# Dealing out a depthwise convolution of 31 taps over GpSimd, VectorE and ScalarE, and moving weight loads to another queue

## The reference

```
u = rms_norm(h) * (1 + scale) + shift
p = u @ w_in                       # q, k, v, za, glu (a and g), zc
q, k = rope_2d(norm per head)      # 8 query heads, 2 key heads, 64 wide
attn = softmax over 2304 keys (256 context + 2048 own) * silu(za)
glu  = a * sigmoid(g)              # 512 channels
conv = depthwise conv of glu, width 31, padding 15, + bias
conv = silu(layer_norm(conv)) @ w_pw + b_pw, times silu(zc)
h = h + gate * ([attn, conv] @ w_out)
```

## Time and profile before

| | us |
|---|---|
| median of 3 runs | 3052.08 (3051.74 to 3052.36) |
| the profiled execution | 3046.05 |
| its span | 3044.2 |
| projections, first turn to last | 1209.3 to 1895.6 |
| attention, first score matmul of step 0 | 1967.7 |

### The profile page before, as it was taken

How to read it: one execution, slowest core, us unless ns; L and a number is a source line. 1 busy time by engine, 2 the same in 40 slices (tenths; PEclk the granted TensorE clock), 3 DMA queues, 4 the chain that set the end, 5 groups by cost and what they waited for, 6 DMA issues and landing times. The chain is left out here.

```text
span 3044.2 us, 35493 instructions
## 1 busy us (share of the span) xinstructions
PE 2615.0 (86%) x11647; PEld 1777.7 (58%) x11647; DVE 1814.0 (60%) x2830; ACT 1092.1 (36%) x1875; POOL 793.3 (26%) x365
## 2 busy tenths in 40 slices
PE   8599899999999962767989797299999999975998
PEld 1277677777777751645767675144454445433776
DVE  0106423533532524698898888677777777746564
ACT  0234433333332413241414132144454445433332
POOL 0033300000000101532111111166566656642000
PEclk9799999999999985888999999599999999987999
DMA  8275664454355341746555554411111111124334
GB/s 307 94 250 167 225 218 143 155 186 164 134 193 193 101 152 59 258 150 228 188 185 202 183 204 157 99 27 26 33 26 28 27 33 26 28 71 149 117 117 148
DMA packets 230581, 414.82 MB, mean 136 GB/s; under 512 B 19607, under 2 KB 112397, under 8 KB 230204
## 3 DMA queue, kind: packets, MB, share of 16 engines
q1 hardware_dynamic: 230096, 413.13, 40.9%
q10 hardware_dynamic: 364, 0.13, 0.0%
HBM read 306.87 MB, written 97.94 MB: 133 GB/s over the span
## 5 line engine op out<-in xcount | busy, mean ns | idle before, releaser
L1694 DVE TENSOR_REDUCE att_mx<-att_bank_m 128x1 f32<-128x512 f32 (+1 forms) x640 | 365.5, 630 | 111.6 <-PE att_bank_m L1558 107.6
L1662 ACT ACTIVATE att_p_f<-att_bank_s 128x512 f32<-128x512 f32 x576 | 317.7, 598 | 288.0 <-PE att_bank_s L1599 281.0
L412 PE MATMUL gla_bank_g<-gla_a_hi,gla_w_hi 128*128 128x512 f32 x1024 | 416.1, 406 | 4.1 <-POOL gla_w_lo L365 3.1
L412 PE MATMUL gla_bank_g<-gla_a_hi,gla_w_lo 128*128 128x512 f32 x1024 | 403.7, 394 | 0.0
L412 PE MATMUL gla_bank_g<-gla_a_lo,gla_w_hi 128*128 128x512 f32 x1024 | 403.7, 394 | 0.0
L1543 POOL TENSOR_TENSOR att_den<-att_den,att_p_f 128x1024 f32<-128x1024 f32 x160 | 379.4, 2371 | 34.1 <-ACT att_p_f L1662 22.0
L1333 DVE SCALAR_TENSOR_TENSOR proj_conv_acc<-proj_conv_in,proj_conv_w,proj_conv_acc 128x528 f32<-128x528 f32 x508 | 383.2, 825 | 0.3
L1196 PE MATMUL proj_bank_g<-proj_u_hi,proj_w_hi 128*128 128x512 f32 x704 | 302.8, 430 | 74.9 <-DMA proj_w_lo<-scratch_w_lo 37.8
L1196 PE MATMUL proj_bank_g<-proj_u_lo,proj_w_hi 128*128 128x512 f32 x704 | 283.5, 403 | 0.0
L1196 PE MATMUL proj_bank_g<-proj_u_hi,proj_w_lo 128*128 128x512 f32 x704 | 282.6, 401 | 0.0
L1573 PE MATMUL att_bank_o<-att_p_f,att_v 128*64 128x512 f32 x1152 | 268.4, 601 | 0.0
(11 more groups left out here) (322 smaller groups left out, 4195.4 us busy)
## 6 DMA issues: line engine op xcount, KB each, us to landing
gla_w_hi<-scratch_w_hi SPq DMA_DIRECT2D x96, 512.0 KB, 3.7
gla_w_lo<-scratch_w_lo SPq DMA_DIRECT2D x96, 512.0 KB, 4.7
proj_w_hi<-scratch_w_hi SPq DMA_DIRECT2D x66, 512.0 KB, 3.9
proj_w_lo<-scratch_w_lo SPq DMA_DIRECT2D x66, 512.0 KB, 5.3
scratch_w_hi<-gla_w_hi SPq DMA_DIRECT2D x32, 512.0 KB, 3.2
scratch_w_lo<-gla_w_lo SPq DMA_DIRECT2D x32, 512.0 KB, 4.2
mod_wslab<-in_ada_w SPq DMA_DIRECT2D x6, 2048.0 KB, 11.2
mod_wslab<-in_w_mod SPq DMA_DIRECT2D x6, 2048.0 KB, 8.1
```

Source lines behind the costliest of these rows:

```text
L412: last = pe.matmul(banks[s % 2][:], w[:, k, :], a[:, k, :], start=(k == 0 and n == 0), stop=(k == KT - 1 and n == 2))
L1662: act.activation(p_f[:, kt, :], S[kt % SBANKS][:], ACT.Exp, scale=float(HD) ** -0.5).then_inc(p_done, 1)
L1694: dve.reduce_max(mx[:, qt, n:n + 1], M[p % MBANKS][:, 0:min(TB, KEYS - TB * n)], AX_X).then_inc(mx_read, 1)
```

## The change

In `projections`:
- Chunk 0 of the convolution goes to GpSimd, 31 taps a block, each a tensor_scalar into `prod` and a tensor_tensor add (the first tap only the former), dealt by POOL_TAPS_OF_TURN. Chunks 1 and 2 stay on VectorE, 512 wide (528 in the last block), 62 a block, 11 of them carried to the next block's first two turns, none in block 0. Chunk 3 is only written to scratch as `conv_u`, with its weights.
- `u_hi` is rounded and biased on ScalarE (`round_u`) instead of VectorE; `scale_h` comes one turn earlier. The work for a block after the last is gone.
- The pairs are loaded from ScalarE's queue (`load_pair`), after ScalarE has waited for the turn that frees the tile, and the rings have four places.
- SP stores three parts of the convolution apart: GpSimd's at turn 21, VectorE's at turn 3, `conv_u` at turn 9.

In `attention`: chunk 3, one tap a step over all 2048 tokens in steps 0 to 30. ScalarE multiplies four parts of 512 at tiles 4, 6, 8 and 13; GpSimd adds once, 128x2048, behind its six denominator adds. The lists of ScalarE and GpSimd are written out, not loops. The result is stored at the end.

```diff
-    TAPS_OF_TURN = [10, 10, 8] + [0] * 2 + [8] * 5 + [2] * 6 + [8] * 4 + [6] * 2
-    CARRIED = sum(TAPS_OF_TURN[:4])
+    RING = 4
+    NTAP = 2 * TAPS
+    POOL_C, DVE_C, LATE_C = 0, 1, 3
+    TAPS_OF_TURN = [6, 5] + [0] * 4 + [7] * 3 + [5] * 2 + [0] * 5 + [2, 3, 3, 4, 5, 3]
+    CARRIED = sum(TAPS_OF_TURN[:6])
+    POOL_TAPS_OF_TURN = [0] * 2 + [2] * 2 + [1] * 4 + [3, 2, 3, 2, 3] + [1] * 6 + [2] * 2
...
                         if j == 20 and b + 2 < NB:
                             sp.wait_ge(u_done, UP + b * 8 + 16)
...
+                        if j == 21:
+                            sp.wait_ge(pool_taps, UP + (b + 1) * TAPS)
+                            sp.dma_start(conv_y[:, POOL_C, ds((b + 1) * TB, window(b))],
+                                         conv_acc[:, POOL_C, 0:window(b)]).then_inc(pool_conv_stored, 16)
+                        if j == 9:
+                            sp.wait_ge(glu, UP + b * 4 + 4)
+                            sp.dma_start(d["conv_u"][:, ds(b * TB, TB)], vraw).then_inc(late_stored, 16)
...
+                                if k == 0:
+                                    pool.tensor_scalar(acc, conv_src(b, POOL_C, k), conv_w[:, POOL_C, 0:1], None, ALU.mult).then_inc(pool_taps, 1)
+                                else:
+                                    pool.tensor_scalar(prod[:, 0:window(b)], conv_src(b, POOL_C, k), conv_w[:, POOL_C, k:k + 1], None,
+                                                       ALU.mult).then_inc(pool_prod, 1)
+                                    pool.wait_ge(pool_prod, UP + b * (TAPS - 1) + k)
+                                    pool.tensor_tensor(acc, acc, prod[:, 0:window(b)], ALU.add).then_inc(pool_taps, 1)
...
+                def load_pair(n):
+                    j = n % NW
+                    if n < NW + RING:
+                        act.wait_ge(w_kept[n % RING], UP + 32 * (n // RING))
+                    if n < 2 * NW:
+                        act.wait_ge(w_kept[j % RING], UP + 32 * (j // RING + 1))
+                    for part, tile in (("w2_hi", w_hi[n % RING]), ("w2_lo", w_lo[n % RING])):
+                        act.dma_start(tile[:].rearrange("p k n -> p (k n)").bitcast(F32), d[part][j]).then_inc(pair_landed[n % RING], 16)
...
+                def round_u(b, k):
+                    act.wait_ge(hm, UP + b * 8 + k + 1)
+                    act.activation(u_hi[b % 2][:, k, :], hbuf[:, k, :], ACT.Identity, bias=modv[:, 1, k:k + 1]).then_inc(u_done_hi, 1)
...
                         act.wait_ge(proj, UP + b * NW + j + 1)
+                        if NW <= b * NW + j + RING < NB * NW:
+                            load_pair(b * NW + j + RING)
...
+    MUL_AT = (4, 6, 8, 13)
...
+                def tap(k):
+                    pool.wait_ge(conv_mul, UP + NB * (k + 1))
+                    if k:
+                        pool.wait_ge(conv_taps, UP + k)
+                    former = conv_prod[:, 0, :, :] if k == 1 else conv_acc[:].rearrange("p (a b) -> p a b", a=NB)
+                    if k == 0:
+                        pool.sem_inc(conv_taps, 1)
+                    else:
+                        pool.tensor_tensor(conv_acc[:].rearrange("p (a b) -> p a b", a=NB), former, conv_prod[:, k % 2, :, :], ALU.add).then_inc(conv_taps, 1)
...
                         pool.tensor_tensor(den[s][:], pair(0) if j == 1 else den[s][:], pair(j), ALU.add).then_inc(den_pool, 1)
-                steps(pool, body)
+                    if i < TAPS:
+                        tap(i)
...
+                    if k > 1:
+                        act.wait_ge(conv_taps, UP + k - 1 + (k == 2))
+                    act.activation(conv_prod[:, k % 2, part, :], conv_in[:, k + TB * part:k + TB * (part + 1)], ACT.Copy,
+                                   scale=conv_w[:, k:k + 1]).then_inc(conv_mul, 1)
```

More of the change, by code:

```diff
@@ L1029, in projections @@
         w_landed = [sem(f"w_landed{s}") for s in range(2)]
[L1030 to L1031 removed]
+        pair_landed = [sem(f"pair_landed{s}") for s in range(RING)]
+        w_kept = [sem(f"w_kept{s}") for s in range(RING)]
         w_rounded, w_rest, proj, evac = sem("w_rounded"), sem("w_rest"), sem("proj"), sem("evac")
@@ L1650, in finish, with multiply @@
                     act.activation(o_hi[:], O[HD:P, :], ACT.Copy).then_inc(o_hi_done, 1)
-                def body(i, s, g, before, after):
+                def multiply(k, part):
+                    if k == 0 and part == 0:
+                        act.wait_ge(conv_landed, UP + 32)
+                        act.wait_ge(conv_cleared, UP + 2)
+                    if k > 1:
+                        act.wait_ge(conv_taps, UP + k - 1 + (k == 2))
+                    act.activation(conv_prod[:, k % 2, part, :], conv_in[:, k + TB * part:k + TB * (part + 1)], ACT.Copy,
+                                   scale=conv_w[:, k:k + 1]).then_inc(conv_mul, 1)
+                round_q(0, 0)
+                act.wait_ge(ones_landed, UP + 16)
+                for g in range(NKV):
+                    act.activation(k_b[g][HD:HD + 1, :], ones[HD:HD + 1, 0:1].broadcast_to([1, KEYS]), ACT.Copy).then_inc(ones_row, 1)
+                round_k(0)
+                round_q(1, 1)
+                for g in range(1, NKV):
+                    round_k(g)
+                read_row(0, 0)
+                for i in range(STEPS):
+                    s = i % 2
+                    before, after = i if i else None, i + 1 if i + 1 < STEPS else None
                     for kt in range(NKT):
@@ L1664, in body @@
                             finish(i - 1, 1 - s)
-                        if kt == 11 and not (isinstance(i, int) and i + 2 >= STEPS):
+                        if kt == 11 and i + 2 < STEPS:
                             round_q(i + 2, s)
@@ L1668, in body @@
                             read_row(i + 1, 1 - s)
-                round_q(0, 0)
-                act.wait_ge(ones_landed, UP + 16)
-                for g in range(NKV):
-                    act.activation(k_b[g][HD:HD + 1, :], ones[HD:HD + 1, 0:1].broadcast_to([1, KEYS]), ACT.Copy).then_inc(ones_row, 1)
-                round_k(0)
-                round_q(1, 1)
-                for g in range(1, NKV):
-                    round_k(g)
-                read_row(0, 0)
-                steps(act, body)
+                        if kt in MUL_AT and i < TAPS:
+                            multiply(i, MUL_AT.index(kt))
                 finish(STEPS - 1, 1)
```

200 lines of the change are left out of this document (113 added, 87 removed).

## The result

| | before | after |
|---|---|---|
| median us | 3051.91 (4 runs) | 3204.32 (4 runs, 3203.35 to 3205.18) |
| span of the profiled execution | 3044.2 | 3202.9 |

The ratio is 1.0501, 95% interval 1.0483 to 1.0519: slower by 5%. The direction was forecast, the size was not: 3082 us was predicted, 30 us more than before, and it became 152, outside the range of 3020 to 3135.

The account below looks back on a forecast made before the run. TensorE was taken to bound the attention, not the projection blocks, where VectorE is busy 140 of 160 us. 3046.05 - 40 + 8 - 2 - 26 + 87 + 3 = 3076, with 6 for the median 3082 us; range 3020 to 3135.

Parts of the forecast that it names:

- The attention, +87: Attention: GpSimd's tap delays VectorE's den adds and the maxima; TensorE waits 2.9 us a step, 30 steps, +87 us.
- The lock: Attention: VectorE and GpSimd operations collide; the first den add ends 1.1 us after the tap.
- Blocks 1 to 3, -40: Projections, blocks 1 to 3: stalls of 93 us fall to 53, so -40 us, bounds -93 and +10.
- I put 50 at block starts: Blocks 1 to 3: 50 us of stalls at block starts go, as pairs no longer stand behind `zout`.
- the collisions: Query turns of the blocks: GpSimd's adds delay VectorE's norms, so the wait grows by about 5 us a block.
- The multiply, 0.7: Projections: GpSimd's multiply by a column takes 0.7 us for 512 columns, between 0.43 and 1.26.
- Rival (c): Projections: GpSimd becomes the bound, multiply as slow as the add, 19 us more a block; 3141 us, chance 0.12.
- Block 0: Projections, first block: GpSimd's chain of 137 us plus 42 of VectorE delay ends at 1418; +8 us, bounds -35 and +35.
- The gap and the start: Stretch between blocks and attention: -26 us, between -15 and -30; start of block 0: -2 us.
- The store at the end: Behind the attention: a 1 MB store replaces a small one, +3 us.
- (b): Rival, attention: no price, VectorE hides the tap; 2995 us, chance 0.08.

Follow-up runs that it names:

- Experiment 2: Kernel after, with six more pairs of score matmuls at tile 4 of steps 1 to 30, while TensorE would wait: 3075.19 us, ratio 1.0083.
- 3: Kernel after without GpSimd's 29 later chunk 3 adds in the attention, plus seven VectorE additions behind each step's fold: 3222.23 us, ratio 1.0556.
- experiments 7: Kernel before with only the weight pairs moved to ScalarE's queue, three places, convolution untouched: 3046.9 us, ratio 0.9987.
- 8: Version with the attention's tap moved behind the next step's fold, pairs on SP's queue: four places 3011.78 us, three places 3025.44; ScalarE's queue, three places: 3009.96.
- Experiment 9: Version with the attention's tap moved behind the next step's fold (3012.56 us), GpSimd's column multiplies of chunk 0 left out: 2974.33 us, ratio 0.9748.
- experiment 4: Kernel after with GpSimd's attention add narrowed from 2048 columns: half 3006.65 us, ratio 0.986; three quarters 3102.78 us, ratio 1.0161.
- 5: Kernel after with GpSimd's complete attention add moved behind the next step's fold: 3012.56 us, ratio 0.9875.

## Why the prediction was right in direction and wrong in size

- **The attention, +87: the failed step.** "It waits 1.9 us, then 1.0 more: 2.9 us a step ... 30 x 2.9 = +87 us." Tap (4.52 predicted, 4.59 measured), collision and end of the fold came as worked out, and the two waits are 2.5 us a step, 74 in all. The failed step is that the price ended with the wait. It took for granted that TensorE goes on at the speed of the earlier trace rows (0.99) when the wait is over; it goes on at half speed, for 10 us a step on average, which costs 4.9 us a step more, 148 us in all. Experiment 2 (no wait on TensorE, same lock: clock back) and 3 (no lock, same wait: clock gone) show it from both sides. The profile of before held a hint that wasn't used: where TensorE is stalled for a good part, in the blocks, its granted clock is 0.84 to 0.95.
- **The lock.** VectorE's add, issued in the tap, ends 1.09 us after it (1.1 assumed). The Trainium skill ("SBUF — State Buffer", "SBUF: two separate sides") calls the port pair an exclusive lock held for the whole instruction; of a two-input add this is nearly what the rows show, with 0.14 us of the 1.23 hidden.
- **Blocks 1 to 3, -40: right sum and parts, half of the reason wrong.** "I put 50 at block starts", for the pairs that stand behind `zout`. The starts did clear, by 50 us (turns 0 and 1 of block 2: 23.2 us, now 10.9), and the rest of the blocks grew by 13 us (10 forecast). But by experiments 7 and 8 the pairs are some 15 us of the 50, and that only with VectorE light. Behind SP's 13.19 us in the stores stood VectorE, whose busy 140 of 160 us hid that it was 2.6 us a turn too slow in turns 16 to 19. And the collisions came as said: turn 13 grew from 14.4 to 17.9 us in block 2.
- **The multiply, 0.7: wrong, 1.89 us**, above the upper bound (1.26, the two-input form). Where VectorE does nothing meanwhile it takes 1.57 us (at 1444.05, for one), so the term is short by 0.9 us alone and by 0.3 more beside VectorE. GpSimd's groups in the whole span:

```profile
L1188 POOL TENSOR_SCALAR proj_prod<-proj_conv_in,proj_conv_w 128x512 f32<-128x512 f32 x90 | 171.0, 1900 | 5.1
...
L1191 POOL TENSOR_TENSOR proj_conv_acc<-proj_conv_acc,proj_prod 128x512 f32<-128x512 f32 x90 | 126.2, 1403 | 7.5
```

  Rival (c) had 19 us more a block for a multiply as slow as the add, and no block shorter. Yet blocks 1 to 3 were 3 us off the forecast. Experiment 9 prices the multiplies at 38 us in all, so the fit there is in part luck; which term made up for them in blocks 1 to 3 is not shown.
- **Block 0: right by luck.** It grew by 10.3 us (8 forecast), but two errors cancel. The chain of GpSimd was put at 137 us of work and 42 us of delay by VectorE, 180 in all, and GpSimd is busy 179.95 us. But the taps without delays are some 88 us (31 of 1.57 + 1.26), not 67, and the rows leave only some 23 us for delays (the multiplies took 1.89 us, 1.57 alone; the adds 1.40, 1.26 alone; the remainders 2.57, put at 2.4; 17 others 1.6, put at 1.3).
- **The gap and the start**: as worked out, within 2.5 us (-28.0 and -4.4, forecast -26 and -2). The store at the end cost nothing, not 3.
- **Rivals.** None held the time. (b), no price in the attention, at 2995, is what the change is worth once the tap is placed and divided rightly (2990.9).

## What to carry to other kernels

Where TensorE runs at a granted clock of 0.99, price a new wait on it twice: the wait, and half of the time at half clock behind it, which here was 1.8 to 2 times the waits where the clock fell. Waits of 0.3 us a step (experiment 4) and of 0.9 us in one piece (5) cost no clock, two that made 1.4 us cost 2.5 us more, two that made 2.5 us cost 4.9 more; spare matmuls in the wait, or the work moved to the other side of the step, get it back. And before a wait is put down to a queue, look at what would be late next if it were gone: moved alone, the queue gave 2.5 us of the 50 that stood at the block starts.

## What the runs showed of the hardware

- GpSimd's multiply by a column is slower than its two-input add on the same 512 columns (1.90 and 1.40 us; 1.57 and 1.26 with VectorE idle). The Trainium skill ("GPSIMD Engine Reference", "4.1 Engine selection") has it the other way round, with one input about as fast as VectorE and two inputs half as fast; here the measurement decides.
- Yet the multiply doesn't hold VectorE for its length. Ten VectorE taps (0.685 us each alone) beside GpSimd's chain of multiply and add; VectorE's row first:

```profile
1616.64 12.16 DVE L1375 SCALAR_TENSOR_TENSOR proj_conv_acc<-proj_conv_in,proj_conv_w,proj_conv_acc 128x512 f32<-128x512 f32 x10
```
```profile
1617.86 2.01 POOL L1188 TENSOR_SCALAR proj_prod<-proj_conv_in,proj_conv_w 128x512 f32<-128x512 f32 x1
1619.95 1.39 POOL L1191 TENSOR_TENSOR proj_conv_acc<-proj_conv_acc,proj_prod 128x512 f32<-128x512 f32 x1
1621.43 1.89 POOL L1188 TENSOR_SCALAR proj_prod<-proj_conv_in,proj_conv_w 128x512 f32<-128x512 f32 x1
```

  A pair comes every 3.5 us, and 2.83 us of it are the two operations as they take alone (1.57 and 1.26). Taking turns throughout, the 12.16 us would leave VectorE some 2.3, and its ten taps are 6.85 us of work. So, by this estimate, at least 4 us ran beside each other.
- The half clock lasted longer than what led to it: after waits of 2.5 us TensorE ran at half for 6.8 to 13.7 us while it was busy in 98% of the time.
